# Moving the matmul operands of the 384-column passes by 64 bytes in SBUF

## The reference: what is computed

```
def sqrelu_mlp(h, w1, w2):
    return jnp.square(jax.nn.relu(h @ w1)) @ w2
...
    for layer in range(DEPTH):
        hx = rms_norm(x, norm1_g[layer]) * (1 + mod_x[1]) + mod_x[0]
        hc = rms_norm(s_c, norm1_g[layer]) * (1 + mod_c[1]) + mod_c[0]
...
        x = x + mod_x[2] * y_x
        x = x + mod_x[5] * sqrelu_mlp(rms_norm(x, norm2_g[layer]) * (1 + mod_x[4]) + mod_x[3], mlp_w1[layer], mlp_w2[layer])
```

## The kernel before

| operand | stage | passes | offset before |
|---|---|---|---|
| `h0` | input of layer 0's projections | 384, at the start 256 and 512 | 0 |
| `mixa`, `mixb` | input of layer 0's output projection | 384, 256, 512 | 0 |
| `mixc` | the same, k = 3 and 4 | 384, 256, 512 | 320 |
| `h1` | input of layer 0's MLP | 384, at the start 256 and 512 | 0 |
| `hid0` | its hidden units | 384, at the end 256 and 512 | 0 |
| `h2` latent part (`h_lat`) | layer 1 | 512 | 0 |
| `h2` context part (`h_ctx`) | layer 1 | 256 | 192 |
| `ao`, `hid1`, `h3` (`h`), `ms`, `hid2`, `hs` | everything later | 512, 256 | 0 |

## Time and profile before

### The profile page before, as it was taken

One profiled execution on the slowest core, in us unless ns is written; L12 is line 12 of the kernel. 1 busy time (PEld: TensorE's weight loads), 2 busy tenths in 40 slices (PEclk: granted clock), 3 DMA queues, 4 the chain that ended last, 5 costly groups with the idle time before them and its releaser, 6 DMA issues.

```text
span 2518.7 us, 36244 instructions
## 1 busy us (share of the span) xinstructions
PE 2499.4 (99%) x14058; PEld 2217.3 (88%) x14058; DVE 1611.8 (64%) x2519; ACT 969.8 (39%) x1451; POOL 117.9 (5%) x211
## 2 busy tenths in 40 slices
PE   9999999999999999999999999999999999999998
PEld 6999999999999988779888888898888888888887
DVE  5777657764546567766655565766667877644446
ACT  6243533131212245774332243453232464533224
POOL 0000000100000000000100000010001000000000
PEclk9999999999999999999999999999999999999999
DMA  7333313433333321002545553324546323132322
GB/s 288 110 109 109 125 51 134 167 117 102 115 108 126 126 67 59 1 2 84 201 144 174 175 187 118 109 84 163 196 155 222 134 97 109 68 100 93 100 96 97
DMA packets 83964, 303.70 MB, mean 121 GB/s; under 512 B 9200, under 2 KB 11376, under 8 KB 83568
## 3 DMA queue, kind: packets, MB, share of 16 engines
q1 hardware_dynamic: 58336, 208.92, 24.2%
q0 software_dynamic: 25488, 92.81, 10.9%
HBM read 299.60 MB, written 2.10 MB: 120 GB/s over the span
## 4 chain that ended last, share of the span: by engine, by line
PE 97%; DMA 1%; DVE 1%; ACT 1%; SPq 0%; issue 0%; ACTq 0%; DVEq 0%
PE G L685 21%; PE G L687 21%; PE G L686 20%; PE G L712 5%; PE G L714 5%; PE G L713 5%; PE G L779 2%; PE G L780 2%; PE G L781 2%; PE B L1283 2%; PE G L864 1%; PE G L866 1%; PE G L865 1%; PE B L1259 1%; PE G L1243 1%; PE G L1259 1%
## 5 line engine op out<-in xcount | busy, mean ns | idle before, releaser
L1431 ACT ACTIVATE Whi<-Wraw 128x1024 fp32r<-128x1024 f32 x333 | 349.7, 1052 | 418.2 <-DMA Wraw<-wstream_dram 404.7
L2079 DVE TENSOR_TENSOR Wlo<-Wraw,Whi 128x1024 fp32r<-128x1024 f32 x333 | 406.9, 1222 | 117.5 <-ACT Whi L1431 116.4
L685 PE MATMUL G<-h_hi,Whi 128*128 128x384 f32 (+1 forms) x896 | 310.8, 347 | 0.4 <-DVE Wlo L2079 0.3
L687 PE MATMUL G<-h_hi,Wlo 128*128 128x384 f32 (+1 forms) x896 | 308.9, 345 | 0.0
L686 PE MATMUL G<-h_lo,Whi 128*128 128x384 f32 (+1 forms) x896 | 308.9, 345 | 0.0
L686 PE MATMUL G<-hid_lo,Whi 128*128 128x512 f32 (+1 forms) x760 | 276.3, 364 | 0.0
L687 PE MATMUL G<-hid_hi,Wlo 128*128 128x512 f32 (+1 forms) x760 | 276.3, 364 | 0.0
L685 PE MATMUL G<-hid_hi,Whi 128*128 128x512 f32 (+1 forms) x760 | 276.3, 364 | 0.0
L685 PE MATMUL G<-hs_hi,Whi 128*128 128x512 f32 x672 | 264.2, 393 | 0.0
L687 PE MATMUL G<-hs_hi,Wlo 128*128 128x512 f32 x672 | 261.6, 389 | 0.0
L686 PE MATMUL G<-hs_lo,Whi 128*128 128x512 f32 x672 | 261.5, 389 | 0.0
(11 more groups left out here) (596 smaller groups left out, 4971.7 us busy)
## 6 DMA issues: line engine op xcount, KB each, us to landing
Wraw<-wstream_dram SPq DMA_DIRECT2D x333, 512.0 KB, 3.3
Araw<-adaw_dram POOLq DMA_DIRECT2D x176, 512.0 KB, 3.8
Eraw<-wstream_dram SPq DMA_DIRECT2D x22, 512.0 KB, 4.3
FIRST<-firstw_dram SPq DMA_DIRECT2D x6, 1024.0 KB, 19.1
X<-xin_dram SPq DMA_DIRECT2D x4, 768.0 KB, 7.0
X<-xin_dram SPq DMA_DIRECT2D x2, 1536.0 KB, 7.4
out_dram<-X SPq DMA_DIRECT2D x16, 128.0 KB, 1.8
ROW<-rows_dram SPq DMA_DIRECT2D x2, 768.0 KB, 6.4
```

Of the source, the lines that this page charges most:

```text
L685: pe.matmul(o, wh, hi[:, a:b], start=(k == 0), stop=False)
L687: last = pe.matmul(o, wl, hi[:, a:b], start=False, stop=(k == kt - 1))
L1431: act.activation(hi, raw, ACT.Copy).then_inc(w_hi, 1)
L2079: dve.tensor_tensor(lo, raw, hi.bitcast(F32), ALU.subtract).then_inc(w_lo, 1)
```

## The change

Three filler buffers get smaller. `h0_line` and `mixa_line` go from 32 to 16 words and `h1_line` from 48 to 32, each 64 bytes less. `h0`, `mixa`, `mixb` and `h1` move 64 bytes down, and so does `hid0`, which is stacked on `h1`. Their offset becomes 448 instead of 0. `mixc` (320) and all buffers of later stages stay where they are. No instruction, wait or DMA is added, removed or reordered.

```diff
-        h0 = whole("h0", 32, p1)
+        h0 = whole("h0", 16, p1)
         p1.close()
         p2 = ExitStack()
-        sb("mixa_line", [P, 32], where=p2)
+        sb("mixa_line", [P, 16], where=p2)
...
         p4 = ExitStack()
-        h1 = whole("h1", 48, p4)
+        h1 = whole("h1", 32, p4)
         hid0 = whole("hid0", 128, p4)
```

## The result

The changed kernel takes 2523.8 us in the median of 21 runs (2519.71 to 2532.28), the kernel before 2520.63 us in the median of 21 runs beside them (2518.51 to 2522.04). The ratio of the two sets is 1.002, with a 95% interval of 1.0014 to 1.0027. The medians lie 3.2 us apart and the means 5.1 us, since the longest runs of the changed kernel pull its mean up. So the change costs 3 to 5 us, which is small, but the interval excludes no change. The forecast was 2510. Its sign was wrong, and the time lies inside the range.

A forecast was written before the change was run, and what follows sets the result against it. TensorE, busy for 99% of the span, was taken to bound the kernel. 4560 moved passes x 2.3 ns = 10.5 us off the profiled 2520.4 gave 2509.9, forecast 2510 us; 8 in 10 range 2491 to 2536.

The forecast's parts named there:

- the writes: ScalarE and VectorE writing into the moved buffers: same shapes, slack on both engines, put at nothing.
- the rest of 13.3 ns: Time of each TensorE pass above one column per cycle, at 256 or 384 columns; only this could depend on operand place.
- The rival that no address matters: In the moved passes, the rest could be a fixed cost; time stays 2520.7 us; chance 0.20.
- The gap of N/2.4 + 2.5 ns: Skill's warm matmul gap: 162.5 ns at 384 columns, leaving at most 10.8 ns a pass, 49 us; not in the sum.
- the price of a pass at 448: In all 4560 moved passes: 2.3 ns less each at offset 448, 10.5 us in sum.
- The context rows at 192: 256-column context passes at offset 192: 117.7 and 113.5 ns against 120.0 at offset 0, so 2.3 and 6.5 ns less.
- The upper bound of 4.7 ns: Most a moved pass could lose, from five passes at offset 0 after a break, 178 ns each; would give 2542 us.
- larger gain: Moved passes settle as in the later context stretch, 6.5 ns less: 29.6 us, 2491 us; chance 0.18.
- slower rival: Moved streams start 64 bytes behind the weight load and meet it: 3.4 ns more a pass, 15.5 us, 2536 us; chance 0.30.

The follow-up runs named there:

- the doubled step: The changed kernel with h0, mixa, mixb, h1 and hid0 moved another 64 bytes down, to offset 384: 2530.37 us (6 runs), ratio 1.004.
- the probe: Kernels of matmul passes alone, network left out, operands at 64-byte, later 16-byte steps; rest at offset 0 was 13.3 ns at 256, 384 and 512 columns.
- the profiled execution of after: The first profiled execution of the changed kernel, with no further edit: 2521.71 us, one of its two quickest runs.
- the kernel with five small matmuls: The changed kernel with five one-column matmuls ahead of the first pass of the MLP's 384-column stream: median 2531.99 us (ten runs), ratio 1.004.

## Why the prediction was wrong

**What held.** TensorE bounds the kernel, a changed spacing reaches the end one for one within what the runs can tell (the doubled step: 11.1 us by spacing, 11.8 between the profiled executions, 10.0 between the medians), and the writes and the second stage cost nothing. Only the rest of 13.3 ns moved, between 6.7 and 23.3 ns in all that was run. That one address can have several costs and a stream settles to one of them was right too, and it turned out to be what decides. The rival that no address matters fell with the doubled step. By the two sections of the Trainium skill quoted with that rival ("SBUF — State Buffer", Who interferes with whom, and "TensorE: Matmul & The Clock Gate", Step-by-step: what each phase is for) it could not have: there PE waits on no one, and loading the next weights takes no read bandwidth from the running matmul. The runs show 176.0 against 173.3 ns from the operand's place, and 17.8 against 13.3 from that of `Wlo` alone. The gap of N/2.4 + 2.5 ns that the prediction quotes from the Trainium skill ("TensorE: Matmul & The Clock Gate", Back-to-back issue gap) is given there for an isolated matmul and not for a stream with a weight load for each, so it doesn't say what such a stream could reach. Here the lowest level of a long stream at 384 columns is the old 13.3.

**The step that failed** is the price of a pass at 448, 2.3 ns less. At 384 columns, the width of 4152 of the 4560 passes, it measured 0, 1.3 or 3.3 ns more, by the level. It was taken from 256-column passes of the context operand, on the thought that offset alone matters. Two things in it were wrong.

- Width decides the sign. At the very same place (192 modulo 256) 256 columns are at 6.7 or 11.1, 384 at 13.3, 14.7 or 16.7, and 512 at 20.0. The context rows at 192 are in fact the very place of 448 modulo 256, not far from it as I wrote, but in the wrong width. Their 117.7 and 113.5 ns are the rests 11.0 and 6.8, the same two levels that the probe shows.
- The offset counts modulo 256, not 512. So `mixc` at 320 stands at 64, where 384 columns cost the same as at 0. Its six passes at 171.7 ns were too few to tell: 0.01 us of rounding at either end is up to 1.7 ns a pass, as much as the 1.6 that I read, and the stream was mixed from two offsets. Over all its 71 passes with 384 columns `mixc` had a rest of 12.6 before.

The upper bound of 4.7 ns held at 384 columns and was large as a size: it is how a stream starts, and the settled levels at 448 are at most 3.3 above 13.3. At 512 columns it did not hold: a settled stream there is 6.7 above, and the 206 border passes of that width rose by 3.3 on the mean.

**The larger gain and the slower rival.** The 6.5 ns less exist, but at 256 columns alone, and there they are worth 0.7 us. The slower rival had the sign and, with 3.4 ns, the size of the highest level. Of its mechanism, a stream that starts 64 bytes behind the load and meets it, one thing holds: 64 bytes upward costs nothing and 64 downward does. But a meeting in the first columns of every pass would cost any width, and 256 columns are quicker at 448 than at 0. Nor does who starts ahead order the levels at 384 columns: 15.6 at 16 bytes, 13.3 at 224 (32 behind), 20.0 at 240 (16 behind). What it is in SBUF that makes these levels was not shown.

**Where the 3.2 us come from.** From start to start, in the profiled executions: h at 384 columns outside the MLP adds 0.9 us, the output projection of layer 0 adds 0.4 (its 275 passes of 384 columns from 294 to 342 us went from 14.0 to 15.3 ns), the border passes of 512 columns add 206 x 3.3 ns = 0.7, and those of 256 take 205 x 3.4 ns = 0.7 away. That is 1.3 us, and the profiled execution of after is 2521.71 - 2520.42 = 1.3 us longer, with its MLP at 13.3. To this the MLP adds 0, 3.8 or 9.4 us by the level of its stream. Three profiles of the same program show the first two levels. The third, 16.7, was seen in the kernel with five small matmuls, whose profiled execution took 2531.78 us; four runs of the changed kernel lie where it would put them, at 2531.0 to 2532.3. Which level each run outside the profiles had is inferred from its time, and between 2522 and 2524 us the time alone does not tell, since what comes ahead of the MLP varies by a microsecond or two. The measured median is the middle of this mixture and not the cost of any one thing. That the time fell inside the range was luck in part: the range was wide enough for either sign, and no case in it was a mixture of levels.

**What stays open**: how often each level comes; what in the start of a stream picks it; and why the kernel that moved only the MLP's operands has nine of its eleven runs below 2521.5, where the full change has one of 21 there. The 1.3 us of the projections explain a part of that. The MLP has the same addresses in both, and what TensorE does ahead of it differs; a start that depends on that would do the rest, but no run tested it.

## What to carry to other kernels

A row bounds a cost only for its own shape. Before a spacing at another address is carried over, ask for the same number of columns, the same place modulo the true period, and a stretch long enough that 0.01 us of rounding is small against the difference. Where one program can settle to several levels, a single profile tells one of them: look at the spread of the run times first, and profile again when they form groups. And for streams of matmuls with a weight load each, operands and weights that lie whole multiples of 256 bytes apart are the safe choice here: of all offsets tried it is the only one that gave 13.3 ns in every start at both 384 and 512 columns. At 256 columns alone it is among the dearest (13.3, where 112 bytes gave 6.7 in the probe), but no kernel here got that gain.

## What the hardware showed

- A pass of 384 columns takes 176.7 ns behind one transpose and 173.3 on the same bytes behind two. The level holds for all 2831 passes of a stream of 490 us.
- The rest above one column per cycle runs from 6.7 ns (256 columns at 112) to 23.3 (512 columns at 240, in two starts of four), changes with steps of 16 bytes, and repeats every 256 bytes in the eight offsets where that was run.
- 512 columns at 192 cost 6.7 ns more than at 0, and 256 columns in the same place 6.7 less in three starts of four.
- Moving `Wlo` alone, with all operands left in place, costs 4.5 ns a pass at 512 columns (17.8 against 13.3, with `Wlo` at 64 or 128).
